# x in column halves around the first weight half, and constants and norm rows issued later in the first pass

## The reference, cut to what matters

```python
def first_block(x, ...):
    for l in range(2):
        x = layer_norm(ALPHA * x + 0.5 * swiglu(x, ffn_wg[l, 0], ffn_wu[l, 0], ffn_wd[l, 0]), ln_g[l, 0], ln_b[l, 0])
        x = layer_norm(ALPHA * x + token_mix(x, ...), ln_g[l, 1], ln_b[l, 1])
        x = layer_norm(ALPHA * x + 0.5 * swiglu(x, ffn_wg[l, 1], ffn_wu[l, 1], ffn_wd[l, 1]), ln_g[l, 2], ln_b[l, 2])
# swiglu(x, wg, wu, wd) = (silu(x @ wg) * (x @ wu)) @ wd, wg and wu 1024 x 2816, wd 2816 x 1024
# second_block: mod = silu(c) @ ada_w[i] + ada_b[i] shifts, scales and gates an mLSTM, a swiglu, an S5 and a mixture of 8 experts
```

## Time and profile before

| | |
|---|---|
| Median of 3 runs | 2376.51 us (2375.15 to 2378.09) |
| Profiled execution | 2373.5 us |
| Its span in the trace | 2371.6 us |
| PE busy | 2308.7 us, 97% |
| DVE busy | 1793.9 us, 76% |
| ACT busy | 1291.4 us, 54% |
| POOL busy | 180.7 us, 8% |
| DMA | 596.86 MB, mean 252 GB/s |
| Chain that ended last | PE 89%, DVE 6%, ACT 2%, DMA 2% |

### The profile page before, as it was taken

How to read it: one execution, slowest core, us unless ns; L and a number is a source line. 1 busy time by engine, 2 the same in 40 slices (tenths; PEclk the granted TensorE clock), 3 DMA queues, 4 the chain that set the end, 5 groups by cost and what they waited for, 6 DMA issues and landing times.

```text
span 2371.6 us, 32893 instructions
## 1 busy us (share of the span) xinstructions
PE 2308.7 (97%) x12929; PEld 1908.9 (80%) x12929; DVE 1793.9 (76%) x2006; ACT 1291.4 (54%) x1374; POOL 180.7 (8%) x212
## 2 busy tenths in 40 slices
PE   8999999999999999999999998899999999999997
PEld 7788878878888788879877886678888888888875
DVE  5873478868863678778585568869998989899978
ACT  4343444434332643444544447647777778778774
POOL 1100000101100000000010005500000000000010
PEclk9999999999999999999999997999999999999999
DMA  9778369758758377754145543259999999999995
GB/s 358 259 260 172 89 189 299 272 195 290 244 212 180 108 247 250 261 185 149 72 149 197 192 154 117 73 189 359 372 373 380 379 373 384 378 372 383 377 374 203
DMA packets 306852, 596.86 MB, mean 252 GB/s; under 512 B 62184, under 2 KB 97838, under 8 KB 306606
## 3 DMA queue, kind: packets, MB, share of 16 engines
q1 hardware_dynamic: 286004, 521.11, 62.6%
q0 software_dynamic: 20304, 73.98, 9.1%
q10 hardware_dynamic: 428, 0.15, 0.0%
HBM read 589.38 MB, written 5.78 MB: 251 GB/s over the span
## 4 chain that ended last, share of the span: by engine, by line
PE 89%; DVE 6%; ACT 2%; DMA 2%; issue 1%; POOL 0%; SPq 0%; ACTq 0%; DVEq 0%
PE psum L992 19%; PE psum L993 19%; PE psum L1025 13%; PE psum L1142 6%; PE psum L1584 3%; PE psum L1041 3%; PE psum L1591 3%; PE psum L1159 2%; PE psum L3257 2%; PE psum L985 1%; PE psum L987 1%; PE psum L986 1%; DMA ring<-in_moe_w 1%; PE psum L2340 1%; PE psum L2343 1%; PE psum L2341 1%
## 5 line engine op out<-in xcount | busy, mean ns | idle before, releaser
L1245 DVE TENSOR_TENSOR ring_r<-ring,ring_r 128x2048 fp32r<-128x2048 f32 x286 | 652.7, 2289 | 180.3 <-ACT ring_r L1239 180.0
L1239 ACT CAST ring_r<-ring 128x2048 fp32r<-128x2048 f32 x286 | 546.6, 1912 | 382.6 <-PE psum L1025 186.2
L1245 DVE TENSOR_TENSOR ring_r<-ring,tail_r 128x2048 fp32r<-128x2048 f32 x143 | 327.4, 2289 | 95.4 <-ACT tail_r L1239 95.1
L1239 ACT CAST tail_r<-ring 128x2048 fp32r<-128x2048 f32 x143 | 273.4, 1912 | 148.5 <-PE psum L1142 68.2
L992 PE MATMUL psum<-ring_r,arena_r 128*128 128x512 f32 (+1 forms) x872 | 334.8, 387 | 2.8 <-DVE arena_r L1332 2.1
L993 PE MATMUL psum<-ring_r,arena_r 128*128 128x512 f32 (+1 forms) x872 | 331.1, 382 | 0.0
L992 PE MATMUL psum<-ring_r,xT_r 128*128 128x512 f32 (+1 forms) x576 | 216.6, 382 | 3.4 <-ACT ring_r L1239 3.4
L993 PE MATMUL psum<-ring_r,z_r 128*128 128x512 f32 (+1 forms) x576 | 213.6, 376 | 0.0
L1025 PE MATMUL psum<-ring_r,z_r 128*128 128x512 f32 (+1 forms) x864 | 194.8, 369 | 0.0
L992 PEld LDWEIGHTS psum<-ring_r,arena_r 128*128 128x128 f32 x872 | 164.1, 188 | 35.0 <-DVE arena_r L1332 3.3
L993 PEld LDWEIGHTS psum<-ring_r,arena_r 128*128 128x128 f32 x872 | 164.2, 188 | 30.6
(11 more groups left out here) (583 smaller groups left out, 3745.1 us busy)
## 6 DMA issues: line engine op xcount, KB each, us to landing
ring<-in_moe_w SPq DMA_DIRECT2D x264, 1024.0 KB, 7.3
arena<-in_ada_w POOLq DMA_DIRECT2D x48, 1024.0 KB, 10.0
ring<-in_ffn_wg SPq DMA_DIRECT2D x44, 1024.0 KB, 7.5
ring<-in_ffn_wu SPq DMA_DIRECT2D x44, 1024.0 KB, 7.8
ring<-in_ffn_wd SPq DMA_DIRECT2D x44, 1024.0 KB, 7.1
ring<-in_ffn_w SPq DMA_DIRECT2D x33, 1024.0 KB, 5.4
ring<-in_mlstm_w_in SPq DMA_DIRECT2D x8, 2048.0 KB, 8.0
ring<-in_s_w_glu SPq DMA_DIRECT2D x4, 2048.0 KB, 11.3
```

The source lines that it names most:

```text
L1239: act.copy(upper[i % UPPERS], place(PN[r.key, i])).then_inc(upper_ready, 1)
L1245: dve.tensor_tensor(low, raw, upper[i % UPPERS], ALU.subtract).then_inc(lower_ready, 1)
```

## The change

SP's first load is 256 columns of the constants (identity and ones) instead of 128, and x comes as two column halves, the second behind weight half 0. TensorE turns the first column half of both token tiles, does six identity products, waits for the second and turns it; then half 0 begins. ScalarE and VectorE take the first column half, half 0, the second column half, half 1 and half 2 in this order. TensorE's wait before half 0 is for the first column half only, before half 1 for both. The four gate bias loads stay behind half 5 with a semaphore of their own; the rest of `mix_params_sp`, now from column 256 on, is issued behind half 16. POOL issues ln_g and ln_b at its step c = 2 of the first pass instead of ahead of ada_w. TensorE's wait in `mod` for the constants is gone.

```diff
--- before.py
+++ after.py
@@ -300,6 +300,7 @@
     half_landed = [sem(f"half_landed{i}") for i in range(SLOTS - 1)]
     ring_freed = [sem(f"ring_freed{i}") for i in range(SLOTS + 1)]
     x_landed, consts_landed, params_landed = sem("x_landed"), sem("consts_landed"), sem("params_landed")
+    x_rest_landed, gate_bias_landed = sem("x_rest_landed"), sem("gate_bias_landed")
     params_clear = sem("params_clear")
     mix_params_landed, second_params_landed = sem("mix_params_landed"), sem("second_params_landed")
     param_rows = sem("param_rows")
@@ -542,8 +543,11 @@
         count[0] += 16
 
     def start_sp(sp):
-        sp.dma_start(ident, A["consts"][:, 0:P]).then_inc(consts_landed, 16)
-        sp.dma_start(x[:, :, :], A["x"].rearrange("b (t p) d -> p (b t) d", p=P)).then_inc(x_landed, 16)
+        sp.dma_start(consts[:, 0:2 * P], A["consts"][:, 0:2 * P]).then_inc(consts_landed, 16)
+        sp.dma_start(x[:, :, 0:CHUNK], A["x"].rearrange("b (t p) d -> p (b t) d", p=P)[:, :, 0:CHUNK]).then_inc(x_landed, 16)
+
+    def x_rest_sp(sp):
+        sp.dma_start(x[:, :, CHUNK:D], A["x"].rearrange("b (t p) d -> p (b t) d", p=P)[:, :, CHUNK:D]).then_inc(x_rest_landed, 16)
 
     def start_act(act):
         def load(dst, src):
@@ -570,17 +574,21 @@
         for i in range(2):
             load(pe_nat[:, :, i, :], A["cmp_pe"].rearrange("l v j d -> j (l v) d"))
 
-    def mix_params_sp(sp):
-
-        def load(dst, src):
-            load_param(sp, mix_params_landed, NMIX, dst, src)
+    def gate_bias_sp(sp):
 
         ada_b = A["ada_b_2"].rearrange("l (v r f n) -> l v f r n", v=6, f=4, n=P)
-        load(consts[:, P:], A["consts"][:, P:])
         sp.wait_ge(params_clear, 3)
         for l in range(DEPTH):
             for w in range(2):
-                load(gate_rows[0:P:32, 4 * l + 2 * w:4 * l + 2 * w + 2, :], ada_b[l, 2 + 3 * w])
+                sp.dma_start(gate_rows[0:P:32, 4 * l + 2 * w:4 * l + 2 * w + 2, :], ada_b[l, 2 + 3 * w])\
+                  .then_inc(gate_bias_landed, 16)
+
+    def mix_params_sp(sp):
+
+        def load(dst, src):
+            load_param(sp, mix_params_landed, NMIX, dst, src)
+
+        load(consts[:, 2 * P:], A["consts"][:, 2 * P:])
         for i in range(2):
             half = slice(i * HD, (i + 1) * HD)
             load(w2bd[half, :, half], A["cmp_w2"].rearrange("l v i o -> i (l v) o"))
@@ -631,9 +639,15 @@
         pe.wait_ge(consts_landed, 16)
         for _ in range(8):
             pe.matmul(psum[:, 4, 0:P], ident, ident, start=True, stop=True)
-        pe.wait_ge(x_landed, 16)
-        for t in range(NT):
-            turn_x(pe, 0, t)
+        for b, landed_ in enumerate((x_landed, x_rest_landed)):
+            pe.wait_ge(landed_, 16)
+            for t in range(NT):
+                for k in range(4):
+                    last = pe.transpose(psum[:, 2 * t + b, k * P:(k + 1) * P], x[:, t, (4 * b + k) * P:(4 * b + k + 1) * P], ident)
+                last.then_inc(x_turned, 1)
+            if b == 0:
+                for _ in range(6):
+                    pe.matmul(psum[:, 4, 0:P], ident, ident, start=True, stop=True)
 
     def columns_pe(pe):
 
@@ -674,6 +688,18 @@
                 xT[:, 4 * b:4 * b + 4, t * P:(t + 1) * P]
             act.copy(dst, psum[:, i, :].rearrange("p (k n) -> p k n", k=4)).then_inc(xT_ready, 1)
 
+    def copy_first_act(act, b):
+        for t in range(NT):
+            act.wait_ge(x_turned, NT * b + t + 1)
+            act.copy(xh[:, t, 4 * b:4 * b + 4, :], psum[:, 2 * t + b, :].rearrange("p (k n) -> p k n", k=4)).then_inc(xT_ready, 1)
+
+    def split_first_dve(dve, b):
+        for t in range(NT):
+            part = slice(4 * b, 4 * b + 4)
+            dve.wait_ge(xT_ready, NT * b + t + 1)
+            dve.tensor_tensor(xT_r[:, part, t * P:(t + 1) * P], psum[:, 2 * t + b, :].rearrange("p (k n) -> p k n", k=4),
+                              xh[:, t, part, :], ALU.subtract).then_inc(xl_ready, 1)
+
     def modulate(eng, q, i):
 
         l, w = divmod(q - 6, 2)
@@ -730,8 +756,6 @@
 
         if m > 0:
             pool.wait_ge(x_ready, NT * m)
-        else:
-            pool.wait_ge(*landed_half(PN[0, 3]))
         if m < 6:
             g, b = A["ln_g"][m // 3, m % 3], A["ln_b"][m // 3, m % 3]
         else:
@@ -950,9 +974,13 @@
                 k = slice(j * KD // 2, (j + 1) * KD // 2) if c < NC - 1 else slice(0, KD)
                 src = rows(wg if kind == "g" else wu)[:, k, c0:c0 + w]
             load_half(sp, PN[key, i], src, e)
+            if (key, i) == (0, 0):
+                x_rest_sp(sp)
             if (key, i) == (0, 3):
                 columns_sp(sp)
             if (key, i) == (0, 5):
+                gate_bias_sp(sp)
+            if (key, i) == (0, 16):
                 mix_params_sp(sp)
             if (key, i) == (1, 5):
                 second_params_sp(sp)
@@ -1163,7 +1191,6 @@
 
             dst = mod_sums(r, c)
             pe.wait_ge(ada_ready, 2 * (r.n * NC + c + 1))
-            pe.wait_ge(mix_params_landed, NMIX[0])
             for f in range(4):
                 mm = pe.matmul(dst[32 * f:32 * f + 32, :], ones[:, 0:32], ada_acc[:, f * P:(f + 1) * P], start=True, stop=True)
             mm.then_inc(mod_done, 1)
@@ -1190,8 +1217,8 @@
             if i >= UP_HALVES:
                 c = (i - UP_HALVES) // 2
                 pe.wait_ge(hL_ready, r.groups(max(c, NC - 2)) if tiles == NT and c < NC - 1 else r.groups(c))
-            if r.n == 0 and i == 0:
-                pe.wait_ge(xl_ready, 4)
+            if r.n == 0 and i < 2:
+                pe.wait_ge(xl_ready, NT * (i + 1))
             if i == 4 and r.n == 0:
                 pe.wait_ge(param_ready, 4)
             if r.n is not None and r.n > 0 and i < 3:
@@ -1415,7 +1442,7 @@
         if is_gate_piece(i):
             j = 2 * (2 * l + v // 3) + part
             if j == 0:
-                dve.wait_ge(mix_params_landed, NMIX[0])
+                dve.wait_ge(gate_bias_landed, 16 * 4)
             dve.scalar_tensor_tensor(gate_rows[:, j, :], sums, 1.0, gate_rows[:, j, :], ALU.add, ALU.add)\
                .then_inc(mod_ready, 1)
         else:
@@ -1445,6 +1472,10 @@
 
         for c in range(NC):
             i = n * NC + c
+            if i == 0:
+                pool.wait_ge(*landed_half(PN[0, 3]))
+            if i == 2:
+                ln_pool(pool, 0)
             if c == 0:
                 load_ada(pool, i)
             if c < NC - 1:
@@ -3674,8 +3705,6 @@
         start_pool(pool)
         for st in stages:
             if st.startswith("ffn") and int(st[3:]) < 4:
-                if int(st[3:]) == 0:
-                    ln_pool(pool, 0)
                 gate_pool(pool, int(st[3:]))
             elif st == "ffn4" and "s5" in stages:
                 s5_load_b(pool)
@@ -3704,13 +3733,14 @@
     def _(act):
         step = Count(act_step)
         start_act(act)
-        for t in range(NT):
-            copy_xT_act(act, 0, t)
         for st, earlier, later in zip(stages, [""] + stages, stages[1:] + [""]):
             if st.startswith("ffn"):
                 r = Pass(int(st[3:]))
                 if st == "ffn0":
-                    for i in range(3):
+                    copy_first_act(act, 0)
+                    upper_act(act, r, 0)
+                    copy_first_act(act, 1)
+                    for i in range(1, 3):
                         upper_act(act, r, i)
                 ffn_act(act, r)
             elif st.startswith("ln"):
@@ -3792,9 +3822,10 @@
             if st.startswith("ffn"):
                 r = Pass(int(st[3:]))
                 if st == "ffn0":
-                    for t in range(NT):
-                        split_xT_dve(dve, 0, t)
-                    for i in range(3):
+                    split_first_dve(dve, 0)
+                    lower_dve(dve, r, 0)
+                    split_first_dve(dve, 1)
+                    for i in range(1, 3):
                         lower_dve(dve, r, i)
                 ffn_dve(dve, step, r)
             elif st.startswith("ln"):
```

More of the change, by code:

```diff
@@ L571, in columns_sp @@
             load(pe_nat[:, :, i, :], A["cmp_pe"].rearrange("l v j d -> j (l v) d"))
+    def gate_bias_sp(sp):
+        ada_b = A["ada_b_2"].rearrange("l (v r f n) -> l v f r n", v=6, f=4, n=P)
+        sp.wait_ge(params_clear, 3)
+        for l in range(DEPTH):
+            for w in range(2):
+                sp.dma_start(gate_rows[0:P:32, 4 * l + 2 * w:4 * l + 2 * w + 2, :], ada_b[l, 2 + 3 * w])\
+                  .then_inc(gate_bias_landed, 16)
     def mix_params_sp(sp):
@@ L576, in load @@
             load_param(sp, mix_params_landed, NMIX, dst, src)
-        ada_b = A["ada_b_2"].rearrange("l (v r f n) -> l v f r n", v=6, f=4, n=P)
-        load(consts[:, P:], A["consts"][:, P:])
-        sp.wait_ge(params_clear, 3)
-        for l in range(DEPTH):
-            for w in range(2):
-                load(gate_rows[0:P:32, 4 * l + 2 * w:4 * l + 2 * w + 2, :], ada_b[l, 2 + 3 * w])
+        load(consts[:, 2 * P:], A["consts"][:, 2 * P:])
```

## The result

The changed kernel takes 2381.66 us in the median of 11 runs (2378.94 to 2387.52), the kernel before beside it 2376.03 (2372.36 to 2379.64): ratio 1.0024, 95% interval 1.0016 to 1.0032, **slower by 0.24%, 5.6 us**. The forecast was 2376.9, and the result lies above its range. The profiled execution of the changed kernel has a span of 2377.1 us, 5.5 more than before's.

A forecast was written before the change was run, and what follows sets the result against it. The first pass was taken to be bound by TensorE, gaining only in its gaps: -0.75 - 1.7 - 1.5 + 2.7 + 1.7 = +0.4 us on the median 2376.5 gave 2376.9 us, range 2372.0 to 2380.0.

The forecast's parts named there:

- The start, -0.75: Before half 0: x's second half lands at 9.85, so TensorE's first product starts at 10.8 instead of 11.55, -0.75 us.
- The clock, -1.7: During half 0: identity products and transposes fill the idle gap, so TensorE's clock holds, -1.7 us; 0 if it falls.
- The gap at half 8, -1.5: TensorE's entry to half 8: half 9 lands by 40, VectorE's copy is in time, the gap goes, -1.5 us.
- The stall at half 16, +2.7: TensorE's entry to half 16: half 17, behind the late loads, lands at about 105.6, +2.7 us; bounds 0 and 10.8.
- a sign of being wrong: TensorE's gap before half 16: forecast wrong if it is missing or over 5 us, or one opens at halves 3 to 7.
- The turn taking: DMA queues around half 16: q0 and q1 pass packets one for one, holding small packets to 85 per us beside POOL's.
- the hidden rival: At half 16: half 17 lands by 103.1 and no stall comes, 2372.6 us; chance 0.13.
- The clock after the stall, +1.7: Behind the stall at half 16: idle TensorE loses its clock again for a stretch, +1.7 us, bound 0.
- The slower one: SP's queue between halves 16 and 17: small packets' backlog, landing at about 110, stall of 7, over 0.2% slower; chance 0.06.
- stall without the clock: At half 16: the stall comes but the clock does not fall, -1.25 us, 2375.3 us; chance 0.26.
- rival three: At the start: clock falls despite filling, or x's second half lands later; 1.7 missing, 2378.6 us; chance 0.12.
- rival C: Rival in the follow-up runs, at the start: halved x is what costs, 2379 us or above; no chance given.

The follow-up runs named there:

- experiment 8: Changed kernel with constants and small loads behind half 20 and both column halves of x issued before weight half 0: 2374.87 us, ratio 0.9988 to the kernel before.
- experiment 9: Changed kernel with constants and small loads behind half 20 and without the six identity products: 2375.07 us, ratio 0.9991 to the kernel before.
- experiments 1: Changed kernel with constants and small loads again behind half 5 and norm rows again ahead of ada_w (the start alone): 2379.62 us, ratio 1.0011 to the kernel before.
- 3: Kernel before, x whole, no identity products, with only the change's later constants, small loads and norm rows (the late part alone): 2377.93 us, ratio 1.0002.
- experiment 5: Changed kernel with the two norm-row broadcasts back ahead of ada_w, constants and small loads still behind half 16: single time 2375.63 us.
- 14: Second profiled execution of the kernel before with only the change's later constants, small loads and norm rows: span +4.4 us to before's first execution.
- 13: Kernel before, unaltered, third profiled execution: single time 2378.61 us.
- 12: Kernel before, unaltered, second profiled execution: single time 2378.97 us.
- 6: Changed kernel with the small loads back behind half 5, the constants alone behind half 16: single time 2375.23 us.
- experiments 2: Changed kernel with constants and small loads issued behind half 20 instead of half 16, nothing else: 2371.55 us, ratio 0.9977 to the kernel before.

## Why the prediction was wrong

**The places were right, the sum of the sizes was not.** For the first pass, against the same profiled execution, it read: -3.95 to half 8, +4.4 at half 16, together +0.4. The traces give -3.2 and +7.1, together +3.9.

**The start, -0.75: failed.** "The second x half lands at 9.85" was 10.8, so TensorE started at 11.65. The landing moves: with the same start code the first product came at 11.65, 11.27, 11.12, 11.66, 11.44, 11.41, 10.99, 10.98 and 11.33, mean 11.3. The term is +0.1 in the execution that was compared, and -0.35 from mean to mean (before's three start at 11.55, 11.83 and 11.62). Half 0, forecast for 8.3, landed by 9.24. The order of the loads is right (experiment 8), but the arrival of 512 KB was set to the end of its bytes at full rate with 0.15 us on top.

**The clock, -1.7: right against the execution it was read from.** The first half takes 5.55 us for 7.17, and without the products 7.15 again (experiment 9). But in before's other two executions the first half takes 6.93 and 5.56 us: in one the clock did not fall at all. Against their mean the term is -1.0.

**The gap at half 8, -1.5: right in the trace**, by the late part and not by the start (experiments 1 and 3). Against a mean before it is worth more, since the gap there was 1.8 and 3.7 us with low clock in the other two executions. I had only one execution and took its gap for the kernel's.

**The stall at half 16, +2.7: mis-sized, and this is the step that decided.** It measured 5.1 and 5.3, over the 5 that the prediction had named as a sign of being wrong. On the old axis half 17 was to land at 105.6 and landed at 108.2; the 4.54 us behind it came out as 4.53. By the queues' packets 2.4 of the 2.6 us split so (these are positions read by adding up bytes slice by slice, so good to some 0.3 us). Half 16's packets ended at 88.4, 91.6 on the old axis, against 90.7: 0.9 late. Its first packet passed 2.3 us or more after the issue, with q0's norm rows on the DMA engines at 91% in 82 to 83. In before it passed at 85.37, 1.0 us after the issue; the prediction's 1.5 was a misreading. Constants and small packets added 0.2. The bytes of half 17 were through at about 103.0, but ScalarE saw it landed at 104.9, 1.9 us later where I had allowed 0.6: 1.3. What makes up these 1.9 us is not shown; the slices add up all 16 DMA engines, and a single one may have ended later. The turn taking was right where both queues were full, though not in every slice (in 95 to 96 q1 passed 231 packets beside q0's 66). In two slices of one us each, beside the earlier trace rows:

```profile
q0 software_dynamic: 79, 0.32, 93.1%
q1 hardware_dynamic: 77, 0.03, 13.4%
```

```profile
q1 hardware_dynamic: 415, 0.23, 101.0%
q0 software_dynamic: 12, 0.02, 11.5%
```

In 97 to 98 q1 has 77 packets beside q0's 79; in 99 to 100, with q0 at its end, 415. The trace agrees with the Trainium skill (page DMA: Bandwidth & Descriptors, section SWDGE vs HWDGE vs iDMA). But what decided was less the turns than the bytes: 8.3 of the 9.6 us. My forecast had spent the room that was left, from 98 to 102.9, on them already, so each further microsecond of lateness was a microsecond of stall. The sum that was to check this was wrong too: the 6.9 MB set against the hidden rival leave out the small loads. With them it is 7.4 MB, 19.1 us, until 104.5 on bytes alone. So with ada_w ahead of half 17, as the forecast has it, "hidden" was excluded, and the 105.0 for half 17's last packet held only 0.5 us for everything that is not bytes.

**The clock after the stall, +1.7: right**, 1.8 measured.

**The rivals.** The slower one had place and mechanism (backlog before half 17) and put its landing at 110 and the stall at 7; the measured 5.1 lies midway between it and the forecast, and I gave it 6%. "Hidden" and "stall without the clock" did not come; of rival three the part that said x's second half lands too late is true.

**What stays open.** In the first pass, the mean before and the mean change differ by 2.8 us; the medians by 5.6 and 4.4. So 1.6 to 2.8 us of the medians' difference is not explained. The profiled executions don't hold it: behind the store, the span grows against before's first by 0, 3.5 and 2.8 us in the executions of before, by 1.6 and 2.6 in the change, 2.1 in the mean of either, and by -1.1 to 3.0 in the others. The change's profiled 2378.94 us is the lowest of its 11 runs. What varies there is low clock in stages from 1040 on. An estimate from PEclk in windows of 2 us puts its cost between 1040 and 1600 at 20.5, 20.5 and 23.9 us in before, 23.9 twice in the change and 23.9 twice in the version behind half 20, so by this estimate it isn't tied to the loss. Nor is it explained why the late part alone has the change's gap and low clock but a ratio of 1.0002. Its interval reaches up to 1.0012, 2.9 us, so the 2.7 us of its first pass are not excluded; that halved x costs something together with the late part, rival C, isn't either. Only behind half 20 do halved and whole x come out alike (0.9977 and 0.9982).

## What to carry to other kernels

A load moved "late, where nobody waits for it" must be placed by the bytes that are already due there: add the bytes of all queues between the issue and the first transfer that someone waits for, and if they fill the window, each further one is stall; four halves further on the same loads made no gap. A gain at the start lives only if what limits the next entry moves too: here the start alone fed a DMA that then went ahead of the needed one. And one profiled execution can hold the shortest of the gaps: a gap that hangs on a DMA landing should be entered in the sum with a spread.

## What the runs showed of the hardware

- The clock's fall behind an idle stretch was not a matter of its length alone. It stayed at 1.00 behind 2.3 us (experiment 5), 2.7 (14) and 3.0 (13), and fell behind 1.8 (12), 2.2 (9) and 2.7 (3, 6 and 12); behind the gaps of 3.4, 3.7, 4.4, 4.5, 5.1, 5.3 and 5.5 us it fell.
- A load of 16 KB kept SP's queue for 5.17 us at its issue (the row of gla_wa above). The load itself is not the cause: with the norm rows early it took 2.12 us, with the constants early 1.56, so it hangs on what is in the queues ahead of it.
- Six identity products, 1.5 us of otherwise idle TensorE, kept the clock in all ten executions that have them; in the pair of experiments 2 and 9 they were worth 1.8 us.
